# A hybrid decoder layer on eight cores: the mixer's channel norm finished on token rows, transposed back in bfloat16

## The reference

```python
u = a_val * sigmoid(a_gate)                       # (tokens, 512)
ua = causal_depthwise(ctx_a, u, w_dw_a)           # width 31
ua = silu(layer_norm(ua + b_dw_a, ln_conv_g, ln_conv_b))   # norm over the 512 channels
ub = g_b * vb                                     # group B, short gated convolution
out = concatenate([ua, ub], -1) @ w_o + b_o
```

## Time and profile before

| | |
|---|---|
| median of 3 runs (lowest, highest) | 1211.81 us (1210.76, 1212.04) |
| the profiled execution | 1210.81 us |
| its span, slowest core (all cores) | 1209.2 us (1206.8 to 1209.2) |
| TensorE busy | 1195.0 us, 99% |
| VectorE busy | 539.5 us, 45% |
| ScalarE busy | 239.4 us, 20% |
| GpSimd busy | 197.2 us, 16% |
| mean granted TensorE clock of the cores | 0.997 to 0.999 |

### The profile page before, as it was taken

The page is one execution under the profiler, slowest core; times in us unless marked ns, Lnnn a source line. Parts: engine busy times, 40 slices in busy tenths (PEclk is TensorE's granted clock), DMA queues, the critical chain, the costliest instruction groups (busy, mean ns, idle before and its releaser), DMA issues.

```text
span 1209.2 us, 19878 instructions; the slowest of 8 cores (1206.8 to 1209.2 us)
## 1 busy us (share of the span) xinstructions
PE 1195.0 (99%) x7230; PEld 631.6 (52%) x7230; DVE 539.5 (45%) x893; ACT 239.4 (20%) x427; POOL 197.2 (16%) x310
## 2 busy tenths in 40 slices
PE   7999999999999999999999999999999999999997
PEld 4544444455555566655444444455444466666444
DVE  1213226653433465717854434364736532222356
ACT  1111110121122234311021122235320011111000
POOL 1111102310100013312210100113312110000111
PEclk9999999999999999999999999999999999999999
DMA  9798876766756538995245756438994344443032
GB/s 138 115 214 134 150 137 152 149 145 114 121 99 111 128 71 166 198 222 148 93 119 105 118 100 129 101 88 168 192 187 148 105 99 78 84 70 88 21 110 105
DMA packets 61680, 151.75 MB, mean 125 GB/s; under 512 B 7760, under 2 KB 21392, under 8 KB 61568
## 3 DMA queue, kind: packets, MB, share of 16 engines
q0 software_dynamic: 32192, 80.26, 43.2%
q1 hardware_dynamic: 29392, 70.22, 18.3%
HBM read 202.79 MB, written 28.70 MB: 191 GB/s over the span
## 4 chain that ended last, share of the span: by engine, by line
PE 98%; DMA 1%; DVE 0%; issue 0%; DVEq 0%; ACT 0%; POOL 0%; ACTq 0%; POOLq 0%
PE ps L554 51%; PE ps L618 24%; PE ps L706 12%; PE ps L958 5%; PE ps L810 2%; PE ps L429 1%; DMA sb_ring<-wgu 1%; PE ps L636 1%; PE ps L927 1%; PE ps L896 1%; PE ps L624 0%; PE ps L1153 0%; DVEq L166 0%; ACT sb_mv L514 0%; PE ps L950 0%
## 5 line engine op out<-in xcount | busy, mean ns | idle before, releaser
L554 PE MATMUL ps<-sb_xB,sb_ring 128*128 128x352 bf16 (+1 forms) x2112 | 320.1, 310 | 0.0
L554 PE MATMUL ps<-sb_xA,sb_ring 128*128 128x512 bf16 (+1 forms) x1472 | 312.7, 371 | 4.3 <-DMA sb_ring<-wgu 3.8
L561 DVE TENSOR_TENSOR sb_hT<-sb_sg,ps 128x352 bf16<-128x352 f32 (+3 forms) x224 | 129.0, 576 | 413.1 <-PE ps L554 399.3
L618 PE MATMUL ps<-sb_RW,sb_hT 128*128 128x512 bf16 x1364 | 297.0, 379 | 0.0
L554 PEld LDWEIGHTS ps<-sb_xB,sb_ring 128*128 128x128 bf16 x2112 | 205.6, 98 | 108.7 <-issue 3.4
L554 PEld LDWEIGHTS ps<-sb_xA,sb_ring 128*128 128x128 bf16 x1472 | 142.7, 98 | 160.5 <-issue 7.4
L618 PEld LDWEIGHTS ps<-sb_RW,sb_hT 128*128 128x128 bf16 x1364 | 132.8, 98 | 158.2 <-issue 0.2
L559 ACT ACTIVATE sb_sg<-ps 128x352 f32<-128x352 f32 (+3 forms) x224 | 113.7, 507 | 494.9 <-PE ps L554 447.0
L367 POOL DMA_DIRECT2D sb_ring<-wgu x88 | 48.7, 554 | 468.0 <-PE ps L554 442.1
L451 DVE SCALAR_TENSOR_TENSOR sb_xr<-sb_xr,ps 128x1024 f32<-128x1024 f32 x47 | 57.3, 1219 | 99.1 <-PE ps L618 75.8
L459 POOL TENSOR_SCALAR sb_mv<-sb_mv 128x1 f32<-128x1 f32 (+1 forms) x50 | 43.8, 875 | 352.4 <-DVE sb_mv L457 352.4
(11 more groups left out here) (94 smaller groups left out, 610.5 us busy)
## 6 DMA issues: line engine op xcount, KB each, us to landing
sb_ring<-wgu POOLq DMA_DIRECT2D x88, 512.0 KB, 7.7
sb_RW<-wd POOLq DMA_DIRECT2D x33, 512.0 KB, 13.2
sb_wring<-win POOLq DMA_DIRECT2D x40, 256.0 KB, 6.1
sb_RW<-uscr SPq DMA_DIRECT2D x64, 135.0 KB, 7.3
sb_xr<-xp SPq DMA_DIRECT2D x16, 512.0 KB, 9.2
x1s<-sb_xr SPq DMA_DIRECT2D x16, 512.0 KB, 3.8
sb_xr<-x1s SPq DMA_DIRECT2D x16, 512.0 KB, 10.3
x2s<-sb_xr SPq DMA_DIRECT2D x16, 512.0 KB, 8.6
```

The costliest lines, as they stand in the source:

```text
L554: ins = e.matmul(bank(bk, n), lhsT=ring[:, s, c:c + 128], rhs=xcol(k, tok0, n), start=(k == 0), stop=(k == KC - 1))
L561: P.op("dve", lambda e: e.tensor_tensor(out=hT[:, f, l0:l0 + n], in0=sg[:, q, :n], in1=bank(bu, n), op=ALU.mult), reads=[("sg", q)] + pst( ...
L618: ins = e.matmul(ps[:n, (yb + h) * 512:(yb + h + 1) * 512], lhsT=hT[:, f, l0:l0 + n], rhs=wd[:, f, h * 512:(h + 1) * 512], start=(f == 0), ...
```

## The change

The gain and bias of the channel norm are loaded once as a table `lnc` with the same 2 x 512 numbers in each partition. S1b subtracts the mean and multiplies by the gain, straight from PSUM, and then multiplies by the token's scale and adds the bias, both on VectorE in float32; ScalarE then applies Silu to the rows and writes bfloat16 to the new tile `cbf`. S2 transposes these bfloat16 rows with the bfloat16 identity, and one ScalarE copy takes all four chunks to `catA` or `catS`. GpSimd's product L908 is gone. SBUF holds two more tiles (4 KB and 2 KB a partition), and the area that is set aside for the descriptors of GpSimd's transfers is made 8192 bytes a partition.

```diff
@@ -171,7 +171,7 @@
             block.sync(body_for("sp"))
 
 def build_nc():
-    nc = bass.Bass("TRN2", target_bir_lowering=False)
+    nc = bass.Bass("TRN2", target_bir_lowering=False, dynamic_dma_scratch_size=8192)
     dt = nc.dram_tensor
 
     def din(name, shape):
@@ -195,6 +195,7 @@
     wod = din("wo", [D, D])
     lnbc = din("lnbc", [6, 128, D])
     cstd = din("cst", [128, NCST])
+    lncd = din("lnc", [128, 2 * DA])
     bod = din("bo", [1, D])
     identd = din("ident", [128, 128])
     estkd = din("estk", [128, 4, 32])
@@ -245,6 +246,8 @@
         accS = sb("accS", [128, 4, NS], F32)
         catS = sb("catS", [128, KC, NS], BF16)
         dummy = sb("dummy", [128, 8], F32)
+        lnc = sb("lnc", [128, 2, DA], F32)
+        cbf = sb("cbf", [128, 2, DA], BF16)
         neghalf = sb("neghalf", [128, 1], F32)
         three = sb("three", [128, 1], F32)
         hT = sb("hT", [128, NFC, BLK + NS], BF16)
@@ -905,18 +908,20 @@
                                                       op0=ALU.add), reads=[("mvc", m)], writes=[("vec", m)])
                 P.op("pool", lambda e: e.tensor_tensor(out=mvc[:n, m, 2:3], in0=mvc[:n, m, 3:4], in1=neghalf[:n, 0:1],
                                                        op=ALU.pow), reads=[("vec", m), "neghalf"], writes=[("rsc", m)])
-                P.op("pool", lambda e: e.tensor_scalar(out=mvc[:n, m, 3:4], in0=mvc[:n, m, 0:1], scalar1=mvc[:n, m, 2:3],
-                                                       scalar2=-1.0, op0=ALU.mult, op1=ALU.mult),
-                     reads=[("mvc", m), ("rsc", m), ("vec", m)], writes=[("nmc", m)])
                 s1[t] = (bk, m)
 
             def S1b(t):
                 n = tok(t)[1]
                 (bk, m), sl = s1[t], t % 2
                 pv = ps[:n, bk * 512:(bk + 1) * 512]
-                P.op("act", lambda e: e.activation(out=xnc[:n, sl, :], in_=pv, func=AF.Identity,
-                                                   scale=mvc[:n, m, 2:3], bias=mvc[:n, m, 3:4]),
-                     reads=pst(bk) + [("rsc", m), ("nmc", m)] + WR, writes=[("xnc", sl)])
+                P.op("dve", lambda e: e.scalar_tensor_tensor(
+                    out=xnc[:n, sl, :], in0=pv, scalar=mvc[:n, m, 0:1], in1=lnc[:n, 0, :],
+                    op0=ALU.subtract, op1=ALU.mult), reads=pst(bk) + [("mvc", m), "lnc"] + WR, writes=[("xnc", sl)])
+                P.op("dve", lambda e: e.scalar_tensor_tensor(
+                    out=xnc[:n, sl, :], in0=xnc[:n, sl, :], scalar=mvc[:n, m, 2:3], in1=lnc[:n, 1, :],
+                    op0=ALU.mult, op1=ALU.add), reads=[("xnc", sl), ("rsc", m), "lnc"] + WR, writes=[("xnc", sl)])
+                P.op("act", lambda e: e.activation(out=cbf[:n, sl, :], in_=xnc[:n, sl, :], func=AF.Silu),
+                     reads=[("xnc", sl)] + WR, writes=[("cbf", sl)])
 
             def S2(t):
                 n = tok(t)[1]
@@ -924,17 +929,15 @@
 
                 def pe(e):
                     for ch in range(4):
-                        ins = e.transpose(out=ps[:, bk * 512 + ch * n: bk * 512 + (ch + 1) * n],
-                                          in_=xnc[:n, sl, ch * 128:(ch + 1) * 128], identity=ident[:n, :n])
+                        ins = e.transpose(out=psb[:, bk * 1024 + ch * n: bk * 1024 + (ch + 1) * n],
+                                          in_=cbf[:n, sl, ch * 128:(ch + 1) * 128], identity=ident_bf[:n, :n])
                     return ins
-                P.op("pe", pe, reads=[("xnc", sl), "ident"] + WR, writes=pst(bk))
-                for ch in range(4):
-                    dst = catA[:, ch, l0(t):l0(t) + n] if t < 16 else catS[:, ch, :]
-                    wt = ("catA", ch, t % 4) if t < 16 else ("catS", ch)
-                    P.op("act", lambda e, ch=ch, dst=dst: e.activation(
-                        out=dst, in_=ps[:, bk * 512 + ch * n: bk * 512 + (ch + 1) * n],
-                        func=AF.Silu, scale=cc(C_LG + ch), bias=cc(C_LB + ch)),
-                        reads=pst(bk) + ["cst"] + WR, writes=[wt])
+                P.op("pe", pe, reads=[("cbf", sl), "ident_bf"], writes=pst(bk))
+                dst = catA[:, :, l0(t):l0(t) + n] if t < 16 else catS[:, 0:4, :]
+                wt = [("catA", ch, t % 4) if t < 16 else ("catS", ch) for ch in range(4)]
+                P.op("act", lambda e: e.activation(
+                    out=dst, in_=psb[:, bk * 1024: bk * 1024 + 4 * n].rearrange("p (k n) -> p k n", k=4),
+                    func=AF.Identity), reads=pst(bk) + WR, writes=wt)
 
             def S3(t):
                 n = tok(t)[1]
@@ -1132,6 +1135,7 @@
 
         def consts():
             P.op("sp", lambda e: e.dma_start(out=cst[:], in_=cstd), reads=[("hT", 5, 1)], writes=["cst"], dma="c_cst")
+            P.op("sp", lambda e: e.dma_start(out=lnc[:].rearrange("p h c -> p (h c)"), in_=lncd), writes=["lnc"], dma="c_lnc")
             P.op("sp", lambda e: e.dma_start(out=E4[:], in_=estkd), writes=["E4"], dma="c_e4")
             P.op("sp", lambda e: e.dma_start(out=ident[:], in_=identd), writes=["ident"], dma="c_ident")
             load_ln(0)
@@ -1233,6 +1237,8 @@
     out["cst"] = cst
     est = np.zeros((4, 32, 4, 32), f32)
     est[:, np.arange(32), :, np.arange(32)] = 1.0
+    out["lnc"] = np.ascontiguousarray(np.broadcast_to(np.concatenate(
+        [np.asarray(inputs["ln_conv_g"][0], f32), np.asarray(inputs["ln_conv_b"][0], f32)])[None, :], (128, 2 * DA)))
     out["estk"] = np.ascontiguousarray(est.reshape(128, 4, 32))
     out["bo"] = np.ascontiguousarray(np.asarray(inputs["b_o"], f32).reshape(1, D))
     out["ident"] = np.eye(128, dtype=f32)
```

## The result

| | before | after |
|---|---|---|
| median of the runs | 1211.32 us (1210.76 to 1212.04) | 1220.14 us (1218.85 to 1220.82) |
| ratio after / before, 95% interval | | 1.007 [1.0057, 1.0082] |
| busy in the profiled execution | TensorE 98% | TensorE 98%, VectorE 46%, ScalarE 18%, GpSimd 15% |

The changed kernel is 8.8 us slower. The forecast was 3.8 us slower, with a range that ended at 1218.0: the sign and the place of the waits were right, the size was less than half. Where a later ratio and a quotient of medians differ a little, the ratio is the better number: it leaves out disturbed executions, as do the middle cores and the times of experiments 5 and 6. The profiled execution of after took 1220.47 us. The first fence is from its page, of its slowest core (5).

A forecast was written before the change was run, and what follows sets the result against it. TensorE's in-order stream, 98% of the chain of waits, bounds the kernel. Cheaper transposes (-3.5 us) and new stalls (+7.3) sum to +3.8 on the 1211.81 us median: 1215.6 us, range 1209.0 to 1218.0, the forecast's own 1213.8 to 1216.8.

The forecast's parts named there:

- the sign and the place of the waits: Slower overall, by 3.8 us; TensorE waits on S1b's Silu at tiles 0, 1, 8, 9, 10 and 14.
- Bound: TensorE's stream, 98% of the chain of waits: any microsecond removed or stalled there counts in the whole.
- pitch: Second transposes (S2): four take 0.225 us in bfloat16 against 0.44 in float32; 3.5 us less in all.
- durations: New S1b and S2 operations: 0.75 us for each VectorE operation, 0.62 for the Silu, 0.6 for the copy.
- Tiles 0, 1, 8 and 9: Channel norm: S2's input late by 0.7, 1.2, 1.25 and 3.5 us, behind markers or hT products on VectorE.
- Tile 10's 0.2: Channel norm, second unit: S2's input 0.2 us late behind L561, ready at 794.2 against 794.01.
- Tile 14: Channel norm, second unit: S2's input 0.6 us late behind L561, ready at 848.3 against 847.64.
- The clock: Rival: TensorE's clock falls in tile 9's long stall, costing 1.7 us more, time 1217.3; chance 0.2.
- the sum: Whole kernel: -3.5 from TensorE's transposes and +7.3 of stalls give +3.8 us, 1215.6 us.
- the case in which only the markers' waits are left: No-stall rival at tile 9: pair not behind its hT product, leaving 0.7 and 1.25 us, 1210.3; rival's chance 0.15.
- Neither VectorE: Rival: VectorE becomes the bound where layer-norm work is thick; 1218.6 if two S3 wait; chance 0.08.
- the frame of the change: Table lnc's load and the smaller descriptor area: forecast to cost 0, the load's bounds 0 and 1 us.

The follow-up runs named there:

- experiment 5: Changed kernel with the marker on row 17 of hT dropped after the first down part, so xr loads no longer count as its readers: 1218.95 us.
- experiment 6: Changed kernel with 13 unread matmuls of 512 columns ahead of tile 9's transposes back, filling TensorE's wait: 1218.86 us.
- experiment 2: Kernel before with only the transposes back in bfloat16, S1b staying one ScalarE operation: 1208.85 us, ratio 0.9983 to before.
- Experiment 7: Changed kernel with both the row 17 marker dropped and 13 filling matmuls ahead of tile 9's transposes back: 1214.42 us, ratio 1.003 to before.
- experiment 3: Changed kernel with S1b's two VectorE operations emitted right after the statistics, except for tiles 0 and 8: 1210.75 us, ratio 1.0002 to before.
- experiment 4: Changed kernel with S1b's two VectorE operations emitted early for tile 9 alone: 1215.48 us, ratio 1.0042 to before.
- experiment 8: Changed kernel with the transposes back in float32 and the Silu writing float32 in place: 1224.33 us, ratio 1.0097 to before.
- experiment 1: Kernel before with only the lnc table load, two unused tiles and the smaller descriptor area: 1211.08 us, ratio 1.0 to before.
- experiment 10: Kernel before with both sets of transposes in bfloat16 (accA kept in bfloat16), ScalarE chain as before: 1207.62 us, ratio 0.9966 to before.
- the repeat of experiment 2: Kernel before with only the transposes back in bfloat16, run again with a later batch: 1210.28 us, ratio 0.9992 to before.

## Why the prediction was wrong in size

- **Bound, pitch, durations: right.** TensorE's stream is the time. The pitch fell by 0.22 us per tile as read from the earlier trace rows; experiment 2's middle core shows 3.4 of the forecast 3.5. The new operations cost what the nearest rows said.
- **Tiles 0, 1, 8 and 9: right in place and nearly in size.** Forecast 0.7, 1.2, 1.25, 3.5; measured idle 0.34, 0.80, 1.13, 3.36, with 0.16 more each 0.50, 0.96, 1.29, 3.52. Sum 6.3 against 6.65. Tile 10's 0.2 did not come.
- **Tile 14: the first term that was mis-sized.** Forecast "L561 at 844.89 gives 848.3 against 847.64: 0.6 us". The measured wait was 0.88 to 2.88 us, mean 1.8, and 2.82 on the slowest core. I took the start of L561 from the earlier trace rows as a fixed time and did not ask what it had waited for, although the row says it: 2.64 us for the load of x1s. A transfer's landing time isn't a fixed time: before, the product waited for it there on cores 1, 2, 5 and 7 only, 2.64 to 2.89 us; in after on all eight, 2.70 to 4.68 us. While S1b was ScalarE's, this waiting of VectorE (once more at 480.72 us, for 4.08 us) held up nothing of TensorE's. Behind it on the new queue stood the pair. Experiment 5 took the wait away on all cores, and 3.6 us from the middle core with it.
- **The clock: the second, and the larger on the slowest core.** The rival was named, with its row. Its price of 1.7 us holds for a fall of 3.4 us (tile 14 on core 5: 5.30 − 3.62), but at tile 9 cores 4, 5 and 7 stayed low for 6.8 us (core 5: 2.1 + 0.45 = 2.55, the rest of it lay in the wait). Its chance, 0.2, was too low, and it was priced as one fall in one place. Six cores of eight fell after tile 9, three after tile 14, and cores 5 and 6 in both places. The time is that of the slowest of eight cores, which is one that had both: "the slowest sets the time" was written down there and not carried into the sum. With both included, 1210.8 + 3.8 + 2.2 (tile 14) + 4.25 (clock on core 5) would have been 1221.1; measured 1220.47. The Trainium skill, "TensorE: Matmul & The Clock Gate", section "HAM oscillation — how this bites in real kernels", warns of just this, that idle gaps between bursts of matmuls put the clock back to half. The traces agree on six cores of eight, and show that the same gap can leave a core at full clock.
- **Experiment 7 is the check on the sum**: with both of these taken out, +3.3 against +3.8, or against 3.2 without the 0.6 that the sum had for tile 14. The measured waits, 6.3 less the 3.5 of the pitch, give +2.8, and that is what the middle core shows (1210.9 against 1208.1); that the slowest core comes within 0.1 us of the forecast is partly luck.
- **The other rivals.** The pair did stand behind the group's hT product; moved ahead of it (experiment 3), the kernel took 1210.75, close to the 1210.3 that the rival gave for the case in which only the markers' waits are left. Neither VectorE nor the frame of the change was a bound.

## What to carry to other kernels

When an operation moves to another in-order engine, list not only what stands ahead of it there but what each of those waits for; a wait that is hidden today (a transfer, a marker that was never cleared) becomes the path as soon as something urgent queues behind it. Emit such an operation at the point where its inputs are ready, not where its reader needs it: the same instructions cost 9 us or nothing by place alone. And price a long TensorE wait with a fall of the clock behind it, on the core that is unluckiest: in these kernels 27 of the 35 waits for the Silu of 2.2 us and more had one.

## What the runs showed of the hardware

- **The same gap, two outcomes.** Tile 9's wait was 3.35 to 3.45 us on all eight cores of after; cores 0, 1, 4, 5, 6 and 7 fell to 0.50 of full clock for 3.4 us or more, cores 2 and 3 did not. In experiment 5, with the same wait, cores 0, 1 and 3 did not. At tile 14 of after, waits of 2.30, 2.82 and 2.88 us (cores 3, 5, 6) were followed by a fall, those of 0.88 to 1.96 not; in experiment 4, 2.20 to 2.84 were and 2.11 was not; in experiment 8, 3.15 was, 2.50 and 2.96 were not. Nor is the length of the low stretch the same: 3.4 us or 6.8. What decides it is open. Counted over all kernels, 27 of 35 waits for the Silu of 2.2 us or more were followed by a fall, and no shorter one was. The fall can come after TensorE has started again: at tile 14 of core 5 the transposes start at 856.24 us, windows grant 1.00 up to 857 and 0.55 from 857 to 858.
- **Late weights at 540 us.** In most kernels a wd tile had not landed when TensorE came to the down part of block 0, on one to four cores, for 0.3 to 3.4 us; the profiled execution of before has no such wait. That TensorE gets there earlier is not the whole cause: the frame alone (experiment 1), as fast as before, waited 1.4 and 0.8 us on two cores. Here too a fall of the clock can follow: after 2.9, 3.2 and 3.4 us (experiments 5, 7 and 2; 3.4, 6.8 and 3.4 us low), and not after 2.3, 2.6 or 3.0. It takes part of the gain of experiments 2 and 10 in the slowest core. Its cause was not looked for.
- **A lower clock without a wait.** In experiment 10 cores 0 and 1, in experiments 4 and 7 cores 2 and 3, were granted 0.81 of full clock for 4 to 5 us around 500 us; cores 0 and 1 of experiment 10 once more around 852 us for 3.5 us, and cores 2 and 3 in the repeat of experiment 2 around 856 us for 4. It is always two neighbouring cores at once, with no wait of TensorE's there, and a value between the two levels, not a mixture of them: neighbouring windows inside the stretch show the same 0.81. Core 0 of experiment 10:

```profile
498.00:500.00 2.00, 2.00 (x11) 1.07 (x10) 1.47 (x2) 0.00 (x0) 0.00 (x0) 0.81 1.05 136
500.00:502.00 2.00, 2.00 (x13) 1.13 (x12) 1.79 (x4) 0.46 (x1) 0.00 (x0) 0.81 1.05 146
```

  A group of 16 matmuls holds the stream for 2.88 us there (498.83 to 501.71), and for 2.39 us on core 2 of the same execution (497.07 to 499.46), which was granted full clock. No run here tells what that is. It costs 0.7 to 1.6 us per core.
